# Moved roots, sigmoids and low parts, and unread products at the norms and before the inverses, in a three-block kernel

## Time and profile before

| what | value |
|---|---|
| median of three runs | 2187.85 us (2187.85, 2188.01, 2183.99) |
| the profiled execution's own time | 2184.31 us |
| its span, first to last instruction | 2182.5 us |
| mean granted TensorE clock | 0.994 of full |
| DMA moved | 373.09 MB, mean 171 GB/s |

### The profile page before, as it was taken

One profiled execution on the slowest core, in us unless ns is written; L12 is line 12 of the kernel. 1 busy time (PEld: TensorE's weight loads), 2 busy tenths in 40 slices (PEclk: granted clock), 3 DMA queues, 4 the chain that ended last, 5 costly groups with the idle time before them and its releaser, 6 DMA issues.

```text
span 2182.5 us, 39373 instructions
## 1 busy us (share of the span) xinstructions
PE 2113.6 (97%) x15558; PEld 1851.0 (85%) x15558; DVE 1333.4 (61%) x1846; ACT 1150.2 (53%) x1713; POOL 67.8 (3%) x88
## 2 busy tenths in 40 slices
PE   7999999999999999989999999999999998999998
PEld 5888778888888988889998888888998888998887
DVE  3447565565557976667555556555897575756555
ACT  3554754454445576645445445444557663535444
POOL 1000000000000010100000000000001010000000
PEclk9999999999999999999999999999999999999999
DMA  9763255545554545322445555554454430355553
GB/s 389 297 235 117 97 181 192 185 165 201 183 191 138 190 151 176 120 79 86 180 180 200 190 181 187 186 181 156 171 177 152 156 118 37 141 188 189 182 188 125
DMA packets 53458, 373.09 MB, mean 171 GB/s; under 512 B 6320, under 2 KB 6448, under 8 KB 9424
## 3 DMA queue, kind: packets, MB, share of 16 engines
q1 hardware_dynamic: 47808, 342.00, 43.4%
q0 software_dynamic: 5520, 29.23, 3.9%
HBM read 370.10 MB, written 1.11 MB: 170 GB/s over the span
## 4 chain that ended last, share of the span: by engine, by line
PE 85%; DVE 6%; ACT 4%; issue 2%; DMA 1%; POOL 1%; SPq 0%; DVEq 0%; ACTq 0%; POOLq 0%
PE banks L558 14%; PE banks L560 13%; PE banks L559 13%; PE banks L511 9%; PE banks L513 9%; PE banks L512 9%; PE banks L614 4%; DVE LO L2139 2%; ACT HI L1524 1%; PE banks L668 1%; DMA ring<-in_w_stream 1%; PE banks L643 1%; PE banks L644 1%; PE banks L648 1%; PE banks L1298 1%
## 5 line engine op out<-in xcount | busy, mean ns | idle before, releaser
L1524 ACT ACTIVATE HI<-ring 128x1024 fp32r<-128x1024 f32 x606 | 625.8, 1055 | 717.0 <-PE banks L560 394.8
L2133 DVE TENSOR_TENSOR LO<-ring,HI 128x1024 fp32r<-128x1024 f32 x334 | 409.0, 1227 | 368.8 <-ACT HI L1524 368.5
L2139 DVE TENSOR_TENSOR LO<-ring,HI 128x2048 fp32r<-128x2048 f32 x134 | 307.3, 2293 | 206.7 <-ACT HI L1524 206.3
L511 PE MATMUL banks<-UH,HI 128*128 128x256 f32 x1456 | 423.7, 291 | 5.0 <-DVE LO L2139 5.0
L512 PE MATMUL banks<-UL,HI 128*128 128x256 f32 x1456 | 411.7, 283 | 0.0
L513 PE MATMUL banks<-UH,LO 128*128 128x256 f32 x1456 | 411.5, 283 | 0.0
L558 PE MATMUL banks<-HI,UH 128*128 128x512 f32 x896 | 349.1, 390 | 0.9 <-DVE UL L2146 0.9
L560 PE MATMUL banks<-HI,UL 128*128 128x512 f32 x896 | 348.7, 389 | 0.0
L559 PE MATMUL banks<-LO,UH 128*128 128x512 f32 x896 | 348.6, 389 | 0.0
L511 PEld LDWEIGHTS banks<-UH,HI 128*128 128x128 f32 x1456 | 278.6, 191 | 21.5 <-issue 14.9
L512 PEld LDWEIGHTS banks<-UL,HI 128*128 128x128 f32 x1456 | 278.9, 192 | 1.9 <-issue 1.7
(11 more groups left out here) (354 smaller groups left out, 2992.9 us busy)
## 6 DMA issues: line engine op xcount, KB each, us to landing
ring<-in_w_stream SPq DMA_DIRECT2D x315, 1024.0 KB, 4.8
ARENA<-in_ada_stream POOLq DMA_DIRECT2D x16, 1024.0 KB, 7.8
ARENA<-in_ada_stream SPq DMA_DIRECT2D x8, 1024.0 KB, 13.7
GRMS<-cum_rows POOLq DMA_DIRECT2D x16, 256.0 KB, 3.5
ARENA<-in_na_bias POOLq DMA_DIRECT2D x2, 1024.0 KB, 12.9
RMS<-cum_rows POOLq DMA_DIRECT2D x8, 256.0 KB, 3.6
RSTD<-cum_rows POOLq DMA_DIRECT2D x8, 256.0 KB, 3.7
ARENA<-in_ropes POOLq DMA_DIRECT2D x1, 1088.0 KB, 10.1
```

Of the source, the lines that this page charges most:

```text
L511: nc.tensor.matmul(out, lh, rh, start=start, stop=False, **kw)
L1524: nc.scalar.activation(HI[:, q % PARTS, at], ring[:, q % RING, at], ACT.Copy).then_inc(hi_ready, 1)
L2133: nc.vector.tensor_tensor(LO[:, q % PARTS, at], ring[:, q % RING, at], HI[:, q % PARTS, at].bitcast(F32), ALU.subtract).then_inc(lo_ready, 1)
L2139: nc.vector.tensor_tensor(LO[:, q % PARTS, :], ring[:, q % RING, :], HI[:, q % PARTS, :].bitcast(F32), ALU.subtract).then_inc(lo_ready, 2)
```

## The change

On PE: a new helper issues products of the identity with itself, 128x128, into a bank that nobody reads; five before and five after the spread of `NRSTD` at three norms, and eight after the second `first_turn` in each layer; `b1_half(14, 1)` goes ahead of `ada_columns(1)`. On ACT and DVE: sigmoids, roots, reciprocals and panels' high and low parts change places. In the hardware loop of the convolution the low part of panel i+1 now follows the convolution of panel i, while that of the first stands before the loop, so that the loop's own order of work stays as it was. No DMA is added or moved in the program.

```diff
--- before.py
+++ after.py
@@ -539,12 +539,19 @@
                                                   H[:, t, k * P:(k + 1) * P], DIAG[:, t, :], start=True, stop=True)
                     mm.then_inc(turned_done, 1)
 
+            def unread_squares(to, n):
+
+                for _ in range(n):
+                    nc.tensor.matmul(bank[to][:, 0:P], con("ident"), con("ident"), start=True, stop=True)
+
             def spread_scale(n):
 
+                unread_squares(5, 5)
                 pe.wait_ge(nrstd_ready, n + 1)
                 for t in range(2):
                     mm = spread_tokens(bank[3][:, t * P:(t + 1) * P], NRSTD[:, t:t + 1])
                 mm.then_inc(scale_ready, 1)
+                unread_squares(5, 5)
 
             def raw_turns(n, banks):
 
@@ -943,8 +950,8 @@
                     ada_next += 1
                 if 1 <= n <= 6:
                     head_sums(NA_PAIRS + n - 1)
+            b1_half(14, 1)
             ada_columns(1)
-            b1_half(14, 1)
             pe.wait_ge(ropes_loaded, 16)
             head_spread(2)
             b1_half(15, 0)
@@ -1416,6 +1423,8 @@
                 late_panel(3)
                 for g in range(4):
                     first_turn(g)
+                    if g == 1:
+                        unread_squares(0, 8)
                 inverse_u(0)
                 inverse_u(1)
                 inverse_v(0)
@@ -1786,14 +1795,12 @@
                         split(Q_PROJ1 + k // 2 - 4 + PARTS)
                     if k == 9:
                         open_gates(0, 5)
-                    if k == 10:
+                    if k == 11:
                         open_gates(5, 3)
-                    if k == 11:
-                        open_gates(8, 3)
             gate_rows(0)
             heads_high(2)
+            open_gates(8, 8)
             gate_rows(1)
-            open_gates(11, 5)
             for c in range(4):
                 act.wait_ge(merged_ready, c + 1)
                 nc.scalar.activation(UH[:, 2 * c:2 * c + 2, :], U[:, 2 * c:2 * c + 2, :], ACT.Copy).then_inc(uh_ready, 2)
@@ -1831,6 +1838,7 @@
                 act.wait_ge(small_vector, 3 * l + 2)
                 nc.scalar.activation(SMX[:, 2, :], SMX[:, 1, :], ACT.Exp).then_inc(small_scalar, 1)
                 nc.scalar.activation(SMX[:, 7, 0:SP_COLS], pk2("a_log", 0, SP_COLS), ACT.Exp).then_inc(small_scalar, 1)
+                ahead(LQ_WIDE)
                 act.wait_ge(small_vector, 3 * l + 3)
                 nc.scalar.activation(SMX[:, 4, :], SMX[:, 3, :], ACT.Ln).then_inc(small_scalar, 1)
                 nc.scalar.activation(BETA[:, :, :], tiles(SMX[:, 0, :], 2)[:, :, SP_COLS:SMALL],
@@ -1855,7 +1863,8 @@
 
                 j0 = L_CONV - SCAN_CONV - ROUND
                 for j in range(j0):
-                    ahead(LQ_WIDE + j)
+                    if j:
+                        ahead(LQ_WIDE + j)
                     conv_in(j, j % 2)
                     if j >= 1:
                         conv_silu(j - 1)
@@ -1941,8 +1950,8 @@
                                                  ACT.Square).then_inc(qksq_ready, 1)
                     if j % 2 == 0 and j >= 2:
                         group_squares(j // 2 - 1)
-                    if j in (3, 5):
-                        qk_root((j - 3) // 2)
+                    if j in (2, 5):
+                        qk_root(j // 4)
                 split_half(Q_LAYERS + LQ_WIDE + L_CONV + L_ZS - 1 + PARTS, 0, rounds)
                 group_squares(3)
                 split_half(Q_LAYERS + LQ_WIDE + L_CONV + L_ZS - 1 + PARTS, 1, rounds)
@@ -2636,11 +2646,12 @@
 
                 with dve.Fori(0, (L_CONV - SCAN_CONV) // ROUND - 1) as r:
                     for i in range(ROUND):
-                        split(Q_LAYERS + LQ_WIDE + i + PARTS, rounds + r)
                         convolve(ROUND * r + i, i % 2)
+                        split(Q_LAYERS + LQ_WIDE + i + 1 + PARTS, rounds + r)
 
                 def conv_panel(j):
-                    ahead(LQ_WIDE + j)
+                    if j > L_CONV - SCAN_CONV - ROUND:
+                        ahead(LQ_WIDE + j)
                     convolve_tile(j, j % 2, 0)
                     convolve_tile(j, j % 2, 1)
 
@@ -2752,10 +2763,10 @@
                     dve.wait_ge(wide_free, 2 + WIDE0 + L_WIDE * l + L_CONV + j + 1)
                     x_ = CONV[:, 2 * j:2 * j + 2, :]
                     nc.vector.tensor_tensor(x_, x_, tiles(ZT[:, j % 2, :], 2), ALU.mult).then_inc(yg_ready, 1)
-                    if j in (3, 5):
-                        qk_reciprocal((j - 3) // 2)
                     if j >= 4:
                         qk_norm(j - 4)
+                    if j in (2, 5):
+                        qk_reciprocal(j // 4)
                 ahead(LQ_WIDE + L_CONV + L_ZS - 1)
 
                 def late_low(j):
@@ -2894,10 +2905,10 @@
                     branch_low(j, YSL[:, at, :], YSH[:, at, :], CONV[:, at, :])
 
                 for j in range(4):
-                    scan_low(j)
-                    if j == 1:
+                    if j == 0:
                         dve.wait_ge(orms_ready, l + 1)
                         nc.vector.reciprocal(OROOT, OROOT).then_inc(or_ready, 1)
+                    scan_low(j)
                     if j == 3:
                         late_low(L_ZD + L_GATES - END_GATES)
                 for j in range(4):
@@ -2912,11 +2923,13 @@
                         late_low(L_ZD + L_GATES - END_GATES + 1)
                         for i in range(4, 8):
                             scan_low(i)
+                    if j == 2:
+                        late_low(L_ZD + L_GATES - END_GATES + 2)
                 for j in range(4):
                     at = slice(2 * j, 2 * j + 2)
                     branch_low(8 + j, YDL[:, at, :], YDH[:, at, :], QKV[:, at, :])
-                    if j % 2:
-                        late_low(L_ZD + L_GATES - END_GATES + 2 + j // 2)
+                    if j == 3:
+                        late_low(L_ZD + L_GATES - END_GATES + 3)
                 late_low(L_ZD + L_GATES - 1)
 
 
```

## The result

The changed kernel takes **2161.95 us** (median of 4 runs, 2161.07 to 2163.85); the kernel before, on the same chip beside it, takes 2185.92 us (4 runs, 2183.52 to 2188.01). The ratio is 0.9893, interval [0.9878, 0.9907]: 24.0 us faster, where 17.2 were forecast. The direction and the moves were right; what happens to the clock, and the price of an unread product, were not.

A forecast was written before the change was run, and what follows sets the result against it. TensorE, busy 2113.6 of 2182.5 us, was taken as the bound. Moves 13.3, less 0.6 for products, plus 4.5 clock gain made 17.2 us off the 2187.85 median: 2170.5 us predicted, range 2163 to 2179.

The forecast's parts named there:

- the moves: Reordered work at Z panels, first wide panels, last gates and block 1 removes PE waits: 13.3 us in all.
- the price of an unread product: Each product costs PE 0.13 us; the five before each norm's spread delay it 0.2 us, 0.6 us over three norms.
- Z panels: First query/key root and reciprocal at j = 2 remove PE's 2.1 us wait per layer: 4.2 us gain.
- first wide panels: Third wide panel's high and low parts made ahead of the logarithm: 1.2 us per layer, 2.4 in all.
- last gates: Reciprocal ahead of two low parts gains 1.3 us; an earlier low part gains 2.5 us.
- block 1: 24 products cover the modulation-copy wait, gaining 1.1 us; reordered sigmoids and copies at the attention's end gain 1.8.
- the clock gain: Unread products keep PE's clock up in three norm stretches: 4.5 us, bounds 0 and 6.7; nothing taken for the inverses.
- The frame: Whole-kernel baseline: the runs' median 2187.85 us, 3.5 above the profiled execution, moves the forecast from 2167.1 to 2170.6.
- The rule that spoke against the products: Trainium skill's rule: only longer waits lower the clock, so products at norms are only cost; total gain 12.7 us.
- The first (the products don't hold the clock, 2175.1): Rival at the norms: unread products don't hold the clock, time 2175.1 us; chance 0.16.
- The second (waits form again, 2177.3): Rival: ACT or DVE late next, likeliest at projection or later wide panels; half the moves given back, 2177.3 us; chance 0.15.
- The third (DVE falls behind in the convolution, slower): Rival: low part late by a table load in each of 24 convolution panels, 24 us lost, 2194.7 us; chance 0.03.

The follow-up runs named there:

- E: The changed kernel run once more, unaltered, beside its variants: 2162.58 us, ratio 0.9887 to the kernel before.
- C: Changed kernel without the five products ahead of the spread (2164.39 us), or with six (2162.80) or sixteen (2168.83) instead of eight before the inverses.
- D: Changed kernel with second query/key root and reciprocal at j = 4 (2161.30 us), DVE's norm first in each Z panel's turn (2161.67), or both (2161.72).

## Why the prediction was partly right

**The moves: 13.3 forecast, 13.0 measured** (the work part of the kernel with moves alone), 13.4 by the waits that have gone. By parts, with the spread between the two sets of runs of before: Z panels 4.2 against 5.2 to 5.9; first wide panels 2.4 against 2.7 to 3.4; last gates 3.8 against 3.5 to 4.1, the low part 1.9 for 2.5; block 1, 2.9 against 3.1 in the traces. There its two places came out as worked out: the wait of 1.1 us on the modulation copy has gone (the row of 0.6 is the other of its two), so has the 1.0 on L1737 (0.8 in two waits stay), the 0.9 on L2146 has no row, the 1.5 on the second gate-row copy is 1.4. "The second root is worth nothing" held nearly: 2.3 are 1.9.

**The step that failed is the clock gain: "I take two thirds, 4.5 us; bounds 0 and 6.7. For the inverses I take nothing."** The mean clock rose from 0.9933 (21 runs) to 0.9985 (8 runs of the changed kernel), 2(1 - c)S from 29.3 to 6.5 us, at most half of the 22.8 us, **11.4**, as gain (12.7 from the kernels beside each other in E, 0.9927 and 0.9985). At most 4.2 of it came with the moves and 7.2 with the products on top. Three things stood behind the error. First, the falls were taken from the one profiled execution, which had none at the gate rows and the Z panels; kernels with the same instructions up to there fell at 258 in four profiled executions, and at the Z panels four of six without their move fell. Second, it was taken that the moves leave the clock alone, while they take away the stands at just those two places. Third, the eight products were taken to come too early for the inverses' fall; with all parts in place the inverses are at 1.00 in both layers, though C shows that the eight alone don't decide it.

**An unread product was taken at half of its price.** "Sixteen products like them take 2.05 us, 0.13 each" counted entries of the trace as products of the source. At 0.26 the work behind each norm comes 0.48 us later instead of 0.2, and each inverse 0.17 later instead of nothing: 3 x 0.48 + 2 x 0.17 = 1.8 us in all instead of 0.6. The work part says the same: 2162.36 - 3.24 = 2159.1 for the changed kernel, 1.8 above the moves alone.

**The frame.** The 3.5 us between the profiled execution and the median were added to the forecast as fixed. For the most part they were the chance of three runs: over 43 runs on another chip the median of before is 2184.87, and with a fourth run beside the three it is 2185.92. Put together, from the prediction to the measured time: 2170.5 - 6.9 (clock) + 1.2 (price) - 3.0 (frame) + 0.3 (moves) = 2162.1, against 2161.95. The sum closes in part by how the work part is made, which is the time less half of the low time; what does not lean on that are the waits in the traces (13.4), the delays (1.8) and the fall at the gate rows, which cost half of its length.

**The rule that spoke against the products.** The clock rose from 0.9952 to 0.9985, and the time fell by some 5 us, when unread products alone were added to the moves, and no single wait ahead of any of these falls, at gate rows, norms, Z panels or inverses, was over 2.7 us; of all falls only the one at the kernel's end stands behind a longer wait, some 10 us. By the Trainium skill, page "TensorE: Matmul & The Clock Gate", section "HAM oscillation — how this bites in real kernels", which blames longer waits, the products would have been pure cost and the whole worth 12.7 us. The traces disagree. The section counts half of the throttled time as lost; the traces agree, with 1.5 to 1.7 us for the fall of 3.4 us at the gate rows.

**Rivals.** The first (the products don't hold the clock, 2175.1) fell: no norm is low in any of the 11 kernels that have products there. The second (waits form again, 2177.3) fell for this change and is true for the kernels of D. The third (DVE falls behind in the convolution, slower) fell: L2148 is at 0.6 us in all. Of the signs named ahead, "PE busy down by about 4 us" was wrong, since it left out that the unread products are themselves busy time: 92 entries of 0.13 us are 12 us, against at most 11.4 that the clock gives back. Busy time rose by 1.6.

**Still open:** why either set of products alone is worth next to nothing and both 7 us; why six or eight products hold the inverses and sixteen did not; why the clock is lower with the first wide panels' move alone.

## What to carry to other kernels

Where a busy TensorE stands for a microsecond or two several times in a row, price the clock as well as the wait, and read where it falls from several executions, for one shows only some of the places; closing one place leaves the others, at any of which the clock may fall in the next execution. Read the price of an added instruction from the trace's entries and check how many entries one line of the source makes. Test a set of small edits together before dropping any that measures as nothing alone.

## What the runs showed of the hardware that was not expected

The clock falls at different places from one execution to the next, and with it the time: the kernel before ran between 2182.0 and 2189.0 us in 43 runs on one chip, with a mean clock between 0.991 and 0.995; the changed kernel ran between 2161.1 and 2163.9 in eight, at 0.998 or 0.999. Its two profiled executions differ by a fall at the start, 3.5 us long at 23.5, which one has (2163.85 us) and the other has not (2161.21).

TensorE also stands within a group of like products with nothing to wait for. In the kernel with the moves alone, inside the first round of the inverses of layer 0:

```profile
950.79 0.33 PE L1325 MATMUL banks<-CON,ARENA 64*64 64x64 f32 x2 [1.70 <-issue]
```

In the changed kernel the longest there is 1.23 us; in the norms-only kernel it is 2.5, in that with moves and norms 2.7. What makes these stands was not tried.
